# Finishing the convolution branch (LayerNorm, SiLU and gate) in the tail of the input projection instead of in the output phase

## The chip, the cores and the metric

The kernel runs on one core of one Trainium2 chip. The time is device microseconds for one execution. The engines are named as the profile names them: PE is the matrix engine (TensorE, with PEld its weight loads), DVE the vector engine, ACT the scalar engine, POOL GpSimd; SP is the queue from which most DMAs are issued, and POOL's own queue issues some.

## The reference

One decoder block, for 2048 tokens of 1024 channels in float32. The lines that matter here:

```
proj = h @ w_in[l]
a_val, a_glu, a_gate, cq, ckv, k_pe, b_gate, g_a, g_b = jnp.split(proj, split_points, axis=-1)
u = a_val * jax.nn.sigmoid(a_glu)
u = causal_depthwise_conv(u, conv_w[l], conv_b[l])          # 31 taps, per channel
u = jax.nn.silu(layer_norm(u, conv_ln_w[l], conv_ln_b[l]))  # over the 1024 channels
y_a = (u * jax.nn.silu(a_gate)) @ w_conv_out[l]
...
y_b = (o * jax.nn.silu(b_gate)) @ w_attn_out[l]
merged = jax.nn.sigmoid(g_a) * y_a + jax.nn.sigmoid(g_b) * y_b
x = x + gate[:, None, :] * (merged @ w_out[l])
```

Every large matrix product is made in three passes (`split3`, L50 to L54: high by high, high by low, low by high), since both operands are split into a rounded part (`hi`, made on ACT) and its remainder (`lo`, made on POOL or DVE).

## The kernel before, in words

Five phases run one behind the other: setup, projection, value, attention, output. Within a phase each engine has its own program in a fixed order, and semaphores join them; an engine that waits holds up all that stands behind on it.

**Projection.** The channels lie on the 128 partitions, the tokens along the row. A tile is 128 output columns of `w_in` for all 2048 tokens, in four chunks of 512 tokens (`NC_` = 4, `TC` = 512). A chunk is 8 x 3 = 24 matmuls into one of eight PSUM banks, four of them to even tiles and four to odd ones, so a bank has to be read out before the tile after next reaches it. Five tiles of the attention's latents come first (`PRE`); then a loop over `i` = 0..7 runs six kinds of tile: `glu`, `val`, `ga`, `gb`, `agate`, `bgate`. ACT applies sigmoid, copy or SiLU to each chunk while it reads the bank (L575), into `sg` for `glu`, into `u` for `val`, and into the one stage buffer `lat[:, LT - 1]` for the four kinds that SP then stores to DRAM. ACT also rounds the weights of the tile after next (L499) behind each tile, and POOL makes their remainder (L591). POOL multiplies `u` by `sg` (L631), DVE runs the 31 taps of the convolution over `u` into `acc` (L726, L730), and SP stores `acc` to `conv_dram` (L483).

**Output.** The work goes by 96 units of 24 matmuls. Units 0 to 31 (chunks n = 0 to 3, eight units each) are the attention's product, units 32 to 63 (n = 4 to 7) the convolution's, and the last 32 are `w_out`. Each chunk needs an operand of eight 128 x 512 tiles, split on ACT (L1717) and DVE (L1816). For n = 4 to 7 the operand is computed right there, one chunk ahead: load `conv_dram` and `agate_dram`, sum over the eight tiles on DVE (`total`, L1810), mean over the partitions by a matmul with a constant matrix (L1675), subtract (L1829), square on ACT (L1731), sum again (L1810), mean, root (L1733), reciprocal (L1836), scale (L1840), SiLU on ACT (L1736), gate on POOL (L1778), and then the split. DVE does these steps at the units named in `STEP_AT`, between its reads of the output banks (L1855).

## Time and profile before

| what | value |
| --- | --- |
| median of 3 runs | 2790.12 us (2789.72 to 2791.98) |
| the profiled execution, its own time | 2792.73 us |
| its span (first to last instruction) | 2790.9 us, mean granted clock 0.974 |
| PE busy | 2605.0 us (93%) |
| DVE, ACT, POOL busy | 1685.7 (60%), 894.4 (32%), 695.1 us (25%) |
| DMA | 290.44 MB, 104 GB/s over the span |

The span is 1.8 us shorter than the profiled execution's time, which is 0.1% over the median. PE busy in 93% of the span says that time can only come from the 7% where it waits, from slow stretches of its clock, or from fewer matmuls; where the waits lie has to be read stage by stage.

### The profile page before, as it was taken

What the parts mean: (1) busy time and instruction counts of PE and PEld (TensorE: products, weight loads), DVE (VectorE), ACT (ScalarE), POOL (GpSimd) and SP (SyncE); (2) the same over time, 40 slices, a digit from 0 to 9 for tenths busy, and PEclk for the clock granted to TensorE, in tenths of its full rate; (3) what the DMA queues carried; (4) which work ended last, traced back from release to release, by engine and by line L of the source; (5) the groups of instructions that cost most, each with busy time, mean ns of one, the idle gap of its engine ahead of it and who ended that gap; (6) DMA issues with size and microseconds to landing.
All of it is one profiled execution on the core that took longest, in us unless ns stands there. A gap on an engine that the chain in (4) does not pass through costs nothing. (4 is left out here: it accounts for less than half of the span.)

```text
span 2790.9 us, 33714 instructions
## 1 busy us (share of the span) xinstructions
PE 2605.0 (93%) x12185; PEld 2138.1 (77%) x12185; DVE 1685.7 (60%) x1967; ACT 894.4 (32%) x1726; POOL 695.1 (25%) x571
## 2 busy tenths in 40 slices
PE   3699999999999999997899999999999799888998
PEld 3577888888888888885687887888788687666887
DVE  5765647382929384656467767767777226666442
ACT  3432111111111111111255555555555312323221
POOL 1232211121111111121033233233223301543522
PEclk9799999999999999998999999999999899999999
DMA  7143121221212121214712212211210455555642
GB/s 258 52 137 114 53 75 45 75 68 53 68 53 88 55 90 30 90 47 156 227 64 93 103 41 77 103 60 59 103 60 27 143 193 180 177 183 204 217 166 76
DMA packets 199659, 290.44 MB, mean 104 GB/s; under 512 B 16841, under 2 KB 127501, under 8 KB 189612
## 3 DMA queue, kind: packets, MB, share of 16 engines
q1 hardware_dynamic: 198444, 285.41, 31.1%
q0 software_dynamic: 1152, 4.19, 0.5%
q8 instruction: 39, 0.64, 0.1%
q14 instruction: 24, 0.20, 0.0%
HBM read 194.67 MB, written 94.90 MB: 104 GB/s over the span
## 5 line engine op out<-in xcount | busy, mean ns | idle before, releaser
L52 PE MATMUL ps_proj<-h_hi,w_hi 128*128 128x512 f32 x1696 | 666.3, 393 | 10.8 <-POOL w_lo L591 10.8
L53 PE MATMUL ps_proj<-h_lo,w_hi 128*128 128x512 f32 x1696 | 662.5, 391 | 0.0
L54 PE MATMUL ps_proj<-h_hi,w_lo 128*128 128x512 f32 x1696 | 662.3, 391 | 0.0
L730 DVE SCALAR_TENSOR_TENSOR acc<-u,taps_t,acc 128x2048 f32<-128x2048 f32 x240 | 610.1, 2542 | 35.9 <-DVE acc L730 2.4
L591 POOL TENSOR_TENSOR w_lo<-raw,w_hi 128x1024 fp32r<-128x1024 f32 x55 | 169.8, 3088 | 884.6 <-ACT w_hi L499 884.6
L52 PEld LDWEIGHTS ps_proj<-h_hi,w_hi 128*128 128x128 f32 x1696 | 320.2, 189 | 79.1 <-POOL w_lo L591 11.0
L53 PEld LDWEIGHTS ps_proj<-h_lo,w_hi 128*128 128x128 f32 x1696 | 320.3, 189 | 67.8 <-issue 1.7
L54 PEld LDWEIGHTS ps_proj<-h_hi,w_lo 128*128 128x128 f32 x1696 | 320.0, 189 | 66.8
L1459 POOL TENSOR_SCALAR prob<-prob,rinv 128x512 f32<-128x512 f32 (+2 forms) x320 | 196.7, 633 | 355.3 <-DVE rinv L1413 355.2
L1418 DVE TENSOR_TENSOR pt_lo<-ps_t,pt_hi 128x512 fp32r<-128x512 f32 (+1 forms) x320 | 194.4, 610 | 98.8 <-ACT pt_hi L1341 94.6
L575 ACT ACTIVATE lat<-ps_proj 128x512 f32<-128x512 f32 x128 | 76.8, 600 | 547.3 <-PE ps_proj L54 480.6
L1341 ACT ACTIVATE pt_hi<-ps_t 128x512 fp32r<-128x512 f32 (+1 forms) x320 | 169.7, 532 | 240.7 <-PE ps_t L1253 240.7
L726 DVE TENSOR_SCALAR acc<-u,taps_t,prm_t 128x2048 f32<-128x2048 f32 x8 | 10.8, 1347 | 369.9 <-POOL u L631 369.9
L1395 DVE TENSOR_REDUCE nmax<-ps_ring 128x1 f32<-128x512 f32 (+3 forms) x288 | 174.9, 622 | 97.6 <-PE ps_ring L1238 79.0
L52 PE MATMUL o_ps<-o_a_hi,o_w_hi 128*128 128x512 f32 x512 | 207.0, 404 | 11.3 <-DVE o_a_lo L1816 11.3
L1333 ACT ACTIVATE prob<-ps_ring,nbias 128x512 f32<-128x512 f32 (+2 forms) x320 | 195.5, 626 | 38.5 <-DVE nbias L1401 34.1
L53 PE MATMUL o_ps<-o_a_lo,o_w_hi 128*128 128x512 f32 x512 | 201.7, 394 | 0.0
L54 PE MATMUL o_ps<-o_a_hi,o_w_lo 128*128 128x512 f32 x512 | 201.0, 393 | 0.0
L1253 PE MATMUL ps_t<-ident,prob 128*128 128x128 f32 x1088 | 174.1, 276 | 13.0 <-POOL prob L1459 9.5
L1253 PEld LDWEIGHTS ps_t<-ident,prob 128*128 128x128 f32 x1088 | 132.1, 142 | 46.0 <-POOL prob L1459 10.9
L1268 PE MATMUL ps_o<-pt_hi,v_hi 128*128 128x512 f32 (+1 forms) x320 | 141.5, 442 | 0.7 <-DVE bg L1426 0.7
L1855 DVE TENSOR_TENSOR o_y<-o_ps,o_g 128x512 f32<-128x512 f32 x64 | 43.2, 685 | 149.7 <-PE o_ps L54 64.4
(185 smaller groups left out, 4216.7 us busy)
## 6 DMA issues: line engine op xcount, KB each, us to landing
qlat<-qlat_dram SPq DMA_DIRECT2D x32, 1024.0 KB, 5.2
raw<-in_w_in_dram SPq DMA_DIRECT2D x54, 512.0 KB, 6.1
wada<-in_w_ada_dram SPq DMA_DIRECT2D x8, 1024.0 KB, 12.5
ga_dram<-lat SPq DMA_DIRECT2D x8, 1024.0 KB, 5.0
gb_dram<-lat SPq DMA_DIRECT2D x8, 1024.0 KB, 5.0
agate_dram<-lat SPq DMA_DIRECT2D x8, 1024.0 KB, 5.0
bgate_dram<-lat SPq DMA_DIRECT2D x8, 1024.0 KB, 3.9
conv_dram<-acc SPq DMA_DIRECT2D x8, 1024.0 KB, 5.0
```

Source lines behind the costliest of these rows:

```text
L52: pe.matmul(out, wh, xh, start=first, stop=False)
L53: pe.matmul(out, wh, xl, start=False, stop=False)
L54: return pe.matmul(out, wl, xh, start=False, stop=last)
L591: pool.tensor_tensor(w_lo[slot][:], raw[slot][:], w_hi[slot][:].bitcast(F32), ALU.subtract).then_inc(lo_made, 1)
L730: ins = dve.scalar_tensor_tensor(acc[:], u[:, n:n + S], tap(n), acc[:], ALU.mult, ALU.add)
L1253: mm = pe.transpose(ps_t[:, n % 2, b * P:(b + 1) * P], prob[:, x:x + P], k.ident[:])
L1268: pe.matmul(out, v_hi[:, j, :], mh, start=(j == 0), stop=False)
L1333: act.activation(prob[:, x:x + width], ps[:, chunk_no[n, c] % RING, 0:width], ACT.Exp, bias=nbias[:, n:n + 1], accum_out=rsum[:, n, c:c + ...
L1341: act.activation(pt_hi[n % SLOTS][:, s], ps_t[:, n % 2, s], ACT.Copy).then_inc(t_hi, 1)
L1395: ins = dve.tensor_reduce(to, ps[:, chunk_no[n, c] % RING, 0:width], AX.X, ALU.max, negate=True)
L1418: dve.tensor_tensor(pt_lo[n % SLOTS][:, s], ps_t[:, n % 2, s], pt_hi[n % SLOTS][:, s].bitcast(F32), ALU.subtract).then_inc(t_lo, 1)
L1459: pool.tensor_scalar(prob[:, x:x + width], prob[:, x:x + width], rinv[:, n:n + 1], 1.0, ALU.mult, ALU.mult).then_inc(normed, 1)
```

## The change

The convolution branch is finished before the projection ends, and the output phase loads a ready operand from a new DRAM tensor `z_dram`.

- The 48 tiles of the projection keep their number and their work, but not their order: eight rounds of five kinds (`glu`, `val`, `ga`, `gb`, `agate`), then the eight `bgate` tiles as a tail. The hardware loops become straight code. `TAIL` is the number of the first tail tile.
- The multiplication of `val` by `sg` moves from POOL to DVE, which reads `val` from PSUM itself (`convolve`); ACT no longer touches `val`.
- After each convolution DVE updates a running mean over the tiles and a running sum of squared deviations, 2048 tokens wide (`gather`).
- In the tail, PE makes four matmuls for the mean after chunk 1 of tile TAIL + 1 and four for the variance after chunk 1 of tile TAIL + 2; DVE and ACT finish mean and root.
- Then 32 quarter tiles (128 channels x 512 tokens) pass through six pairs of buffers, laid over `u`, `acc` and `sg`: POOL's queue loads a quarter of `conv_dram` and one of `agate_dram`, DVE subtracts and scales, ACT applies SiLU (two quarters behind each chunk of tiles TAIL + 3 to TAIL + 6), DVE gates, SP stores to `z_dram`, eight quarters ahead of the `bgate` store of each tile.
- The output phase loses all LayerNorm steps for n = 4 to 7; those chunks are split like the others.
- Setup's semaphores are cleared and freed at its end, with a barrier of all engines.

```diff
-    PER = 6
-    KINDS = ["glu", "val", "ga", "gb", "agate", "bgate"]
+    KINDS = ["glu", "val", "ga", "gb", "agate"]
+    TILES = [(kind, i) for i in range(H) for kind in KINDS] + [("bgate", i) for i in range(H)]
...
+    TAIL = PRE + H * len(KINDS)
+    Z_SLOTS = 6
+    ZW = TC
+    N_Z = NC_ * H
+    Z_AT = 8
...
+        z_buf = [b[:, n:n + ZW] for b in (u[:, PAD:], acc, sg) for n in range(0, S, ZW)]
+        z_conv, z_gate = z_buf[:Z_SLOTS], z_buf[Z_SLOTS:]
...
+                    if tile >= TAIL + 3:
+                        for h in range(N_Z)[(tile - TAIL - 3) * Z_AT:(tile - TAIL - 2) * Z_AT]:
+                            sp.wait_ge(z_done, h + 1)
+                            sp.dma_start(k.z_dram[z_rows(h), z_cols(h)], z_conv[h % Z_SLOTS]).then_inc(z_out[h % Z_SLOTS], 16)
+                    if kind in OUTS:
+                        store_tile(OUTS[kind][i * P:(i + 1) * P, :], outs_before(tile))
+                    ready = i if kind == "val" and i else H if tile == TAIL + 1 else 0
+                    if ready:
+                        sp.wait_ge(conv_done, ready)
+                        sp.dma_start(k.conv_dram[(ready - 1) * P:ready * P, :], acc[:]).then_inc(conv_out, 16)
...
+                def ln_means():
+                    for c in range(NC_):
+                        act.wait_ge(ln_dev, c + 1)
+                        act.activation(mean[:, chunk(c)], ps[:, NC_ + c, :], ACT.Copy, scale=float(KT)).then_inc(ln_mean, 1)
+                        act.activation(sg[:, chunk(c)], sg[:, chunk(c)], ACT.Square).then_inc(ln_squared, 1)
+                def ln_roots():
+                    for c in range(NC_):
+                        act.wait_ge(ln_var_mm, c + 1)
+                        act.activation(spread[:, chunk(c)], ps[:, c, :], ACT.Sqrt, bias=k.eps[:]).then_inc(ln_root, 1)
+                def silu(h):
+                    i, s = h % H, h % Z_SLOTS
+                    act.wait_ge(z_scaled, h + 1)
+                    act.activation(z_conv[s], z_conv[s], ACT.Silu, scale=k.prm_t[:, R_LNW + i:R_LNW + i + 1],
+                                   bias=k.prm_t[:, R_LNB + i:R_LNB + i + 1]).then_inc(z_silu, 1)
+                silu_at = [(TAIL + 2, 3)] + [(t, c) for t in range(TAIL + 3, N_TILES) for c in range(NC_) for _ in range(2)]
+                for tile in range(PRE, N_TILES):
+                    kind, i = kind_of(tile)
+                    for c in range(NC_):
+                        if kind != "val":
+                            act.wait_ge(chunk_mm, tile * NC_ + c + 1)
+                            dst = sg[:, chunk(c)] if kind == "glu" else stage[:, c, :]
+                            if c == 0 and kind == "glu" and i:
+                                act.wait_ge(val_used, i * NC_)
+                            if c == 0 and kind in OUTS:
+                                act.wait_ge(stored, 16 * (1 + stores_before(tile)))
+                            act.activation(dst, ps[:, tile % 2 * NC_ + c, :], FUNC[kind]).then_inc(chunk_out, 1)
+                        if tile == TAIL + 2 and c == 0:
+                            ln_roots()
+                        for h in range(N_Z):
+                            if silu_at[h] == (tile, c):
+                                silu(h)
+                    if tile + 2 < N_TILES:
+                        split_hi(0, tile % 2, raw_count(tile + 2), (tile + 1) * NC_)
+                    if tile == TAIL + 1:
+                        ln_means()
...
+                def load_z(h):
+                    s = h % Z_SLOTS
+                    if h >= Z_SLOTS:
+                        pool.wait_ge(z_out[s], 16 * (h // Z_SLOTS))
+                    pool.dma_start(z_conv[s], k.conv_dram[z_rows(h), z_cols(h)]).then_inc(z_in[s], 16)
+                    pool.dma_start(z_gate[s], k.agate_dram[z_rows(h), z_cols(h)]).then_inc(z_in[s], 16)
+                for tile in range(PRE, N_TILES):
+                    if tile == TAIL + 2:
+                        pool.wait_ge(conv_out, 16 * H)
+                        pool.wait_ge(stored, last_store("agate"))
+                        pool.wait_ge(stats_done, H)
+                        pool.wait_ge(ln_sum, NC_)
+                    if tile >= TAIL + 2:
+                        for h in range(N_Z)[Z_SLOTS + (tile - TAIL - 3) * Z_AT if tile > TAIL + 2 else 0:
+                                            Z_SLOTS + (tile - TAIL - 2) * Z_AT]:
+                            load_z(h)
+                    if tile + 2 < N_TILES:
+                        split_lo(tile + 3, tile % 2)
...
+                def convolve(i):
+                    for c in range(NC_):
+                        dve.wait_ge(chunk_mm, (PRE + i * len(KINDS) + 1) * NC_ + c + 1)
+                        dve.wait_ge(chunk_out, outs_before(PRE + i * len(KINDS)) + c + 1)
+                        if i and c == 0:
+                            dve.wait_ge(stats_done, i)
+                        dve.tensor_tensor(u[:, PAD + c * TC:PAD + (c + 1) * TC],
+                                          ps[:, (PRE + i * len(KINDS) + 1) % 2 * NC_ + c, :], sg[:, chunk(c)],
+                                          ALU.mult).then_inc(val_used, 1)
...
+                    dve.wait_ge(mean_step, i)
+                    dve.tensor_tensor(dev, acc[:], mean, ALU.subtract).then_inc(dev_done, 1)
+                    dve.wait_ge(dev_done, i)
+                    dve.scalar_tensor_tensor(mean, dev, 1.0 / (i + 1), mean, ALU.mult, ALU.add).then_inc(mean_step, 1)
+                    part_of = i / (i + 1)
+                    if i == 1:
+                        dve.wait_ge(part_hi_out, 16 * (2 * NC_ + 2))
+                        dve.wait_ge(part_lo_out, 16 * (2 * NC_ + 2))
+                        dve.scalar_tensor_tensor(spread, dev, part_of, dev, ALU.mult, ALU.mult).then_inc(stats_done, 1)
+                        return
+                    dve.wait_ge(mean_step, i + 1)
+                    dve.scalar_tensor_tensor(dev, dev, part_of, dev, ALU.mult, ALU.mult).then_inc(dev_squared, 1)
+                    dve.wait_ge(dev_squared, i - 1)
+                    dve.tensor_tensor(spread, spread, dev, ALU.add).then_inc(stats_done, 1)
...
+                def normalise_z(h):
+                    s = h % Z_SLOTS
+                    dve.wait_ge(z_in[s], 32 * (h // Z_SLOTS + 1))
+                    dve.wait_ge(ln_mean, NC_)
+                    dve.tensor_tensor(z_conv[s], z_conv[s], mean[:, z_cols(h)], ALU.subtract).then_inc(z_centred, 1)
+                    dve.wait_ge(z_centred, h + 1)
+                    dve.wait_ge(ln_done, h // H + 1)
+                    dve.tensor_tensor(z_conv[s], z_conv[s], spread[:, z_cols(h)], ALU.mult).then_inc(z_scaled, 1)
+                def gate_z(h):
+                    s = h % Z_SLOTS
+                    dve.wait_ge(z_silu, h + 1)
+                    dve.tensor_tensor(z_conv[s], z_conv[s], z_gate[s], ALU.mult).then_inc(z_done, 1)
+                for i in range(H):
+                    convolve(i)
+                    gather(i)
+                for c in range(NC_):
+                    dve.wait_ge(ln_mm, c + 1)
+                    dve.scalar_tensor_tensor(sg[:, chunk(c)], ps[:, NC_ + c, :], -float(KT), mean[:, chunk(c)], ALU.mult,
+                                             ALU.add).then_inc(ln_dev, 1)
+                for c in range(NC_):
+                    dve.wait_ge(ln_squared, c + 1)
+                    dve.scalar_tensor_tensor(spread[:, chunk(c)], sg[:, chunk(c)], float(KT), spread[:, chunk(c)], ALU.mult,
+                                             ALU.add).then_inc(ln_sum, 1)
+                invert(0)
+                normalise_z(0)
+                for h in range(N_Z):
+                    if h % H == H // 2 and h // H + 1 < NC_:
+                        invert(h // H + 1)
+                    if h + 1 < N_Z:
+                        normalise_z(h + 1)
+                    gate_z(h)
...
+                        if n == TAIL + 2:
+                            pe.wait_ge(ln_mean, c + 1)
+                        if n == TAIL + 3:
+                            pe.wait_ge(ln_root, c + 1)
...
+                        if n == TAIL + 1 and c == 1:
+                            ln_means()
+                        if n == TAIL + 2 and c == 1:
+                            ln_variances()
...
+    SOURCE_AT = {1: (0, 0), **{c: (c - 2, 4) for c in range(2, 2 * N + 2)}}
...
-                def conv_operand(c):
-                    j = c - N
-                    for h in range(2):
-                        t = slice(h * HALF, (h + 1) * HALF)
-                        act.wait_ge(centred, 2 * j + h + 1)
-                        if j and h == 0:
-                            act.wait_ge(lo_done, KT * c)
-                        act.activation(z[:, t, :], v[:, t, :], ACT.Square).then_inc(squared, 1)
-                    act.wait_ge(mean_mm, 2 * j + 2)
-                    act.activation(rstd[:], ps_m[:, 1, :], ACT.Sqrt, bias=k.eps[:]).then_inc(rooted, 1)
-                    for t in range(KT):
-                        act.wait_ge(scaled, 2 * j + t // HALF + 1)
-                        act.activation(z[:, t, :], v[:, t, :], ACT.Silu, scale=k.prm_t[:, R_LNW + t:R_LNW + t + 1],
-                                       bias=k.prm_t[:, R_LNB + t:R_LNB + t + 1]).then_inc(silu_done, 1)
-                    for t in range(KT):
-                        act.wait_ge(z_done, j * KT + t + 1)
-                        operand_hi(c, t, z)
```

The tail on ACT, from the last chunk of tile TAIL + 4 to the weights behind tile TAIL + 5. Each row is an instruction with its line, output and inputs; `lat<-ps_proj` is the read-out of a `bgate` chunk into the stage buffer, `prm_t` marks the SiLU of a quarter, and `w_hi` is a rounding of weights. After the change:

```order
L631 ACTIVATE lat<-ps_proj 128x512
L617 ACTIVATE u<-u,prm_t 128x512 x2
L545 ACTIVATE w_hi<-raw 128x1024
L631 ACTIVATE lat<-ps_proj 128x512
L617 ACTIVATE u<-u,prm_t 128x512
L617 ACTIVATE acc<-acc,prm_t 128x512
L631 ACTIVATE lat<-ps_proj 128x512
L617 ACTIVATE acc<-acc,prm_t 128x512
L617 ACTIVATE u<-u,prm_t 128x512
```

Two SiLUs stand behind each read-out, so a read-out that waits for the stage buffer holds up the quarters, and a quarter that is late holds up the next read-out and the weights of the tile after next. Before, there were read-outs and weights alone.

POOL in the tail, from the remainder of the weights of tile TAIL + 5 on; `L689` and `L690` issue the two loads of a quarter:

```order
L650 TENSOR_TENSOR w_lo<-raw,w_hi 128x1024
L689 DMA u<-conv_dram 128x512
L690 DMA sg<-agate_dram 128x512
L689 DMA u<-conv_dram 128x512
L690 DMA sg<-agate_dram 128x512
L689 DMA acc<-conv_dram 128x512
L690 DMA sg<-agate_dram 128x512
L689 DMA acc<-conv_dram 128x512
L690 DMA sg<-agate_dram 128x512
```

Sixteen such loads stand between one remainder of weights and the next (the first eight are shown), and each waits until the quarter six before it has been stored. Before, only the remainders and the multiplication `u<-u,sg` stood here.

DVE in the output phase for one chunk of the convolution (n = 5), before the change; `o_y<-o_ps` is the read-out of a unit:

```order
L1810 TENSOR_REDUCE o_tot<-o_v 128x512
L1855 TENSOR_TENSOR o_y<-o_ps,o_g 128x512
L1829 TENSOR_TENSOR o_v<-o_v,o_ps_m 128x2048 x2
L1855 TENSOR_TENSOR o_y<-o_ps,o_g 128x512
L1810 TENSOR_REDUCE o_tot<-o_z 128x512
L1855 TENSOR_TENSOR o_y<-o_ps,o_g 128x512
L1836 RECIPROCAL o_tot<-o_tot 128x512
L1840 TENSOR_TENSOR o_v<-o_v,o_tot 128x2048 x2
L1855 TENSOR_TENSOR o_y<-o_ps,o_g 128x512 x2
L1816 TENSOR_TENSOR o_a_lo<-o_z,o_a_hi 128x512 x4
L1855 TENSOR_TENSOR o_y<-o_ps,o_g 128x512
L1816 TENSOR_TENSOR o_a_lo<-o_z,o_a_hi 128x512 x4
```

and after it, where the same stretch reads:

```order
L1898 TENSOR_TENSOR o_a_lo<-o_v,o_a_hi 128x512 x8
L1910 TENSOR_TENSOR o_y<-o_ps,o_g 128x512 x8
L1898 TENSOR_TENSOR o_a_lo<-o_v,o_a_hi 128x512 x8
L1910 TENSOR_TENSOR o_y<-o_ps,o_g 128x512 x8
L1898 TENSOR_TENSOR o_a_lo<-o_v,o_a_hi 128x512 x8
```

All steps of the LayerNorm are gone from it, and the split of a chunk stands in one piece, as it did for n = 0 to 3.

## Rows read from the trace of the kernel before

**Rows 1.** Busy time by stretch: us from the start, PE, PEld, DVE, ACT, POOL, granted clock, DMA.
```profile
270.00:1294.00 1024.00, 1023.96 (x4518) 847.83 (x4516) 618.35 (x248) 178.38 (x255) 178.41 (x55) 1.00 0.21 64
...
2202.00:2332.00 130.00, 129.24 (x563) 106.87 (x564) 41.00 (x55) 24.03 (x38) 16.81 (x8) 0.98 0.63 207
2332.00:2544.00 212.00, 174.43 (x713) 137.33 (x712) 148.28 (x80) 68.20 (x76) 85.04 (x51) 0.92 0.53 179
```
**Rows 2.** PE's own waits in the output phase: who for whom, total us, times, longest.
```profile
PEld o_ps_m L1675 <- DVE o_tot L1810: 41.0, 8, 11.0
PEld o_ps L52 <- POOL o_w_lo L1771: 11.7, 2, 11.4
```
**Rows 3.** The chain that ended last, first convolution chunk: start us, us, what.
```profile
2340.26 7.32 DVE o_tot L1810
2347.62 1.12 PE o_ps_m L1675 x2
...
2357.84 0.82 ACT o_z L1736
```
**Rows 4.** Matmuls of the output phase: durations min/median/max ns, first and last start us.
```profile
L52 PE MATMUL o_ps<-o_a_hi,o_w_hi x512: 387/389/1415, 2202.8 to 2606.5; 128*128 128x512 f32 x171
...
L54 PE MATMUL o_ps<-o_w_hi,o_a_lo x256: 388/389/389, 2607.6 to 2781.2; 128*128 128x512 f32 x128
```
**Rows 5.** Timeline of ACT, projection's loop: start us, us, what, [idle before <-releaser].
```profile
309.36 0.60 ACT L575 ACTIVATE lat<-ps_proj 128x512 f32<-128x512 f32 x1 [4.84 <-PE ps_proj L54]
314.80 0.60 ACT L575 ACTIVATE lat<-ps_proj 128x512 f32<-128x512 f32 x1 [4.84 <-PE ps_proj L54]
315.29 1.05 ACT L499 ACTIVATE w_hi<-raw 128x1024 fp32r<-128x1024 f32 x1
320.61 0.60 ACT L575 ACTIVATE lat<-ps_proj 128x512 f32<-128x512 f32 x1 [4.26 <-DMA ga_dram<-lat]
...
331.12 0.60 ACT L575 ACTIVATE lat<-ps_proj 128x512 f32<-128x512 f32 x1 [4.84 <-PE ps_proj L54]
```
**Rows 6.** Timeline of DVE and SP: the first convolution and its store.
```profile
301.13 1.35 DVE L726 TENSOR_SCALAR acc<-u,taps_t,prm_t 128x2048 f32<-128x2048 f32 x1 [30.71 <-POOL u L631]
...
383.51 0.37 SPq L483 DMA_DIRECT2D conv_dram<-acc  x1
```
**Rows 7.** DVE groups by form: count, busy us, mean ns, idle before.
```profile
L1840 DVE TENSOR_TENSOR o_v<-o_v,o_tot 128x2048 f32<-128x2048 f32 x8 | 18.0, 2287 | 0.1
...
L1836 DVE RECIPROCAL o_tot<-o_tot 128x512 f32<-128x512 f32 x4 | 13.4, 3350 | 4.6 <-ACT o_tot L1733 4.6
```
**Rows 8.** Timeline of DVE and of POOL, two places.
```profile
2236.08 4.90 DVE L1816 TENSOR_TENSOR o_a_lo<-o_v,o_a_hi 128x512 fp32r<-128x512 f32 x8
...
338.18 3.80 POOL L591 TENSOR_TENSOR w_lo<-raw,w_hi 128x1024 fp32r<-128x1024 f32 x1 [18.43 <-ACT w_hi L499]
```
**Rows 9.** Timeline of SP: the projection's last issues, the value phase's first.
```profile
1294.62 0.37 SPq L439 DMA_DIRECT2D bgate_dram<-lat  x1
1297.11 0.37 SPq L483 DMA_DIRECT2D conv_dram<-acc  x1
1301.44 0.95 SPq L827 DMA_DIRECT2D wv_raw<-in_w_ukv_dram  x2
```
**Rows 10.** DMA issues: count, KB each, median us from issue to landing.
```profile
bgate_dram<-lat SPq DMA_DIRECT2D x8, 1024.0 KB, 3.9
...
bg<-bgate_dram SPq DMA_DIRECT2D x32, 256.0 KB, 2.6
...
o_v<-conv_dram SPq DMA_DIRECT2D x8, 1024.0 KB, 7.9
...
o_yb<-yb_dram SPq DMA_DIRECT2D x32, 256.0 KB, 4.6
```
**Rows 11.** Timeline of POOL: its own DMA issues, the first and a later one.
```profile
112.59 1.66 POOL L600 DMA_DIRECT2D wada_gate<-in_w_ada_dram  x1
...
199.25 0.90 POOL L600 DMA_DIRECT2D wada_gate<-in_w_ada_dram  x1
```

272 lines of the change are left out of this document (102 added, 170 removed).

## The prediction

> **What bounds the kernel now.** I read the busy time by stretch first. In the projection (270 to 1294 us) PE is busy for all of it at full clock, while DVE, ACT and POOL have 406, 846 and 846 us to spare [rows 1]. There anything given to them is free as long as it never holds PE up, and anything given to PE is paid in full. In the output phase PE is busy through the attention's product, and from 2332 to 2544 us, where the operands of the convolution are made, it is busy for only 174.4 of 212 us at a mean granted clock of 0.92 [rows 1]. PE's own waits there are 41.0 us before the mean matmuls, for DVE's sums, and 11.7 us for weights that POOL made late [rows 2]. The chain of work that ended last runs through the same steps: a sum of 7.32 us on DVE, a pair of mean matmuls of 1.12 us, SiLU and gate [rows 3].
>
> **How much the output phase can lose.** A chunk takes PE 5.44 us: ACT's read-outs of two chunks one whole tile apart begin at 309.36 and 331.12, so a tile is 21.76 us and a chunk of 24 matmuls a quarter of it [rows 5]. The output phase is 96 such units, 522.2 us. Its matmuls start at 2202.8, and the last starts at 2781.2, 0.2 us before its slot ends: 578.6 us [rows 4]. Of the excess of 56.4 us, 2.4 belong to the slow clock at its beginning (0.98 of 130 us [rows 1]), which stay. That leaves **54 us**, with the eight mean pairs (9 us) in it.
> Does something take their place? Chunks 4 to 7 get the program of chunks 0 to 3, which kept PE waiting for nothing after its start. Their operand loads fall from 3 MB to 1 MB a chunk, and POOL and ACT lose gate, squares and SiLU. The one crowded place is the start of chunk 4, where eight pieces of weights are fetched two per unit from unit 27 on. A piece costs landing, 1.05 us on ACT [rows 5] and 2.4 to 3.8 on POOL [rows 8], two buffers deep, so some 5 us; the eight are done some 43 us after the first is asked for, and PE needs the last 27 + 38 = 65 us after it. Covered by 20 us. I take all 54; the lower bound is 52.
>
> **What the projection gains in work.**
> - Mean and variance: eight matmul pairs move here. A pair lasts 1.12 us alone [rows 3], of which about 0.15 overlaps its neighbour: **8 us** (7.2 to 9), all on PE's path.
> - The mean's return: tile TAIL + 2 may not start before ACT has read the mean of chunk 0. ACT does so behind the last read-out of tile TAIL + 1 and the rounding of weights. The read-out begins about 0.2 us after PE could go on (a matmul takes 389 ns, the next starts 227 ns behind it [rows 4, 5]), the rounding 0.49 after that and takes 1.05, the mean's copy 0.6 [rows 5]: 2.3 us and a semaphore, **2.4 us**. The roots do not cost that: they are made in the middle of tile TAIL + 2 and wanted at its end, 10.9 us later.
> - Barrier and clearing between the phases: the last store of the projection lands at 1297.11 + 3.9 = 1301.0 and the next phase's first issue is at 1301.44 [rows 9, 10], so a barrier is 0.4 us. I take **0.6**, to 1.5.
> - DVE in the rounds: a convolution runs from 301.13 to 383.51, 82.4 us [rows 6], waits and clashes with POOL included. The statistics are four passes of 2048 elements, two at 2.29 [rows 7], two like a tap at about 2.5, with semaphores 9.9, and up to 1 for a clash: 10.8. With the last multiplication (0.9) that is 94 us of the 108.8 us of five tiles. The first chunk of the next `val` comes 92.5 us after the end of the last: DVE is 1.5 us late for it and in time for the next. That costs nothing, since the bank is wanted a tile and a half later. If cover were gone, each us beyond 108.8 would cost eight.
> - The statistics in time: counted from the start of the tail, S0, the eighth `val` ends at -65.3, and the sums are ready at -65.3 + 94.1 = 28.8. PE asks for them after six chunks, at 32.6. In time by 3.8 us.
>
> **The tail, where I expect a new wait.** Per quarter DVE has a subtraction and a scaling that wait for each other (0.68 + 0.05 each, estimated from a run of eight tiles in 4.90 us, so 0.60 each in a row [rows 8]) and a gate (0.60): 2.1 us; per eight quarters 16.5 us, a reciprocal of 3.35 [rows 7] and 2.4 us of standing still while POOL makes weights: 22.3, already a bit over a tile. Then comes the loop that the order on SP and ACT makes. SP stores the `bgate` tile only behind the eighth quarter of that tile; the first read-out of the next tile waits for this store, and its two SiLUs stand behind the read-out, while DVE may work only one quarter ahead. So from the gate of quarter 7 to that of quarter 15 it takes two issues (0.8), the landing b of 1024 KB, read-out and SiLU (0.6 + 0.82 [rows 3, 5]), and then DVE's remaining 18.4 us with 0.3 of semaphores: **20.9 + b**. Between 3.9 us, the same store in a quiet loop, and more than 7.9 us, a load of the same size in the output phase [rows 10], b is nearest to the latter: eight quarters move 6 MB, with weights and `bgate` 7.5 MB, in 29 us some 270 GB/s, over the 207 and 179 of those stretches [rows 1]. I take 8.5: 29.4 us per eight quarters, against PE's 21.76.
> Tile TAIL + 3 ends on PE at 4 x 21.76 + 8 + 2.4 = 97.4; the gate of quarter 7 is done at 99.6, that of 23 at 158.4. POOL may load quarter 29 only when 23 is stored (issue 0.4, landing as `yb` 4.6 [rows 10]), needs two issues of 0.90 [rows 11], and only then makes the weights of the last tile (3.0): 158.4 + 10.1 = 168.5. PE has finished the last tile but one at 7 x 21.76 + 10.4 = 162.7. It waits **5.8 us** (with b = 3.9 not at all; each us of b is two).
> The Trainium skill, DMA: Bandwidth & Descriptors, section Anatomy of one DMA, gives a transfer 2.0 us plus its bytes at 436 GB/s, 4.4 us for this store and 2.6 for a quarter; by it b were 4.4, PE would not wait in the tail, and the sum would be that of rival A. The rows agree where the chip is quiet (3.9, and 2.6 for 256 KB) and not under traffic (7.9) [rows 10].
> - The end: until now the last convolution's store ended the phase (1297.11 + 3.9); now the `bgate` store does, issued at 1294.62, landed at 1298.5 [rows 9, 10]. **2.5 us** are gained. Quarter 31 is done some 24 us after quarter 23, before PE ends.
>
> **Sum.** -54 + 8 + 2.4 + 0.6 + 5.8 - 2.5 = -39.7 us. The profiled execution's 2792.73 us is 0.1% over the median of 2790.12; taken from the median, this gives 2750.
>
> **Rivals.**
> - A, the tail hides everything: b near 3.9. No wait for the last tile, 2790.1 - 45.5 = 2745; with the smallest bounds 2743. For it speaks that 16 transfers of 256 KB are little for queues that moved 207 GB/s without holding PE up. Chance 0.2.
> - B, the quarters are slower still: six pairs of buffers make a round of store, landing, two loads, landing, two DVE passes, SiLU and gate. With 0.4 + 4.6 + 1.8 + 7.9 + 1.5 + 0.8 + 0.7 = 17.7 us a quarter comes every 2.95 us, just behind DVE's share of my loop; if landings double, or an issue takes 1.66 us [rows 11] and b is 12, eight quarters take 33 to 37 us, the last weights come 12 to 20 us late, and the stores behind the last quarter add up to 6: 2757 to 2772. Chance 0.26.
> - C, statistics late: if POOL and DVE clash on every pass, `gather` takes 19 us, PE waits 4.4 us once, 2755. Chance 0.05.
> - D, slower than before: the gain is used up when the last tile's wait passes 5.8 + 39.7 = 45.5 us, that is quarter 23 at 198 and 49 us per eight, 6.1 us per quarter. One mechanism could do it: a store of a quarter stuck in SP's order behind the `bgate` store, so that loads, which wait for it, run in turn and not side by side; one round of buffers would have to take 37 us in place of 17.7. With both at once the time is 2795 or more. Chance 0.04.
>
> **How the numbers follow.** The forecast (2746 to 2756) has 0.45, A 0.2, B 0.26, C 0.05, D 0.04. The range of eight in ten begins at A's bound, 2743, and reaches to B's end, 2772. A measurement of this kernel tells 0.2%, 5.6 us, from no change. Only D is not faster by that: faster 0.94, same 0.02, slower 0.04.
>
> **What would show it.** Right: from the output phase's first matmul to its last some 524 us and no wait on PE over 2 us; in the projection two groups of four mean pairs, a wait of 2 to 3 us before tile TAIL + 2, and one before the last tile for POOL's `w_lo`; eight quarters every 28 to 31 us; `bgate` landings near 8 us in the tail. Wrong: waits of PE for a `val` bank in the rounds (DVE over 108.8 us), or for the sums at S0 + 32.6; waits at the start of chunk 4; or quarters that keep PE's pace, which is A.

## The result, and the profile after

| kernel | median | ratio to before, 95% interval |
| --- | --- | --- |
| before | 2789.92 us (2787.59 to 2791.98, 4 runs) | |
| after | 2743.12 us (2742.82 to 2745.5, 4 runs) | 0.9834 (0.9817 to 0.9851) |

The change saves 46.8 us, 1.7%; 2750 was forecast, 39.7 saved in the sum. The profiled execution of after took 2742.87 us with a span of 2741.1, against 2790.9 before. The spans differ by 49.8 us, 3 more than the medians, because the profiled execution of before was 2.8 us over its median.

Busy time of after by stretch (columns as in [rows 1]): the projection behind the latents, its tail, and the two parts of the output phase.

```profile
270.00:1301.00 1031.00, 1028.79 (x4525) 848.93 (x4525) 821.19 (x416) 189.70 (x262) 183.96 (x110) 1.00 0.28 89
1130.00:1301.00 171.00, 168.79 (x731) 136.83 (x730) 99.62 (x115) 55.44 (x80) 48.63 (x70) 1.00 0.64 212
2207.00:2337.00 130.00, 129.52 (x564) 107.15 (x565) 34.57 (x55) 23.74 (x38) 16.77 (x7) 0.98 0.59 192
2337.00:2549.00 212.00, 212.00 (x937) 175.61 (x936) 60.23 (x79) 35.08 (x53) 68.72 (x42) 1.00 0.67 214
```

The last row answers to the 174.43 busy us of 212 in [rows 1]: the operands of the convolution now cost PE nothing, and its clock stays at full speed. DVE is busy for 821 us in the projection, a third more than the 618 in [rows 1], and PE stood still for only 2.2 us there. The tail moves 212 GB/s over its length, 280 in its middle (1245 to 1273 us).

The matmuls of the output phase, first kind and last (durations, then first and last start):

```profile
L52 PE MATMUL o_ps<-o_a_hi,o_w_hi x512: 387/389/766, 2207.5 to 2556.8; 128*128 128x512 f32 x171
...
L54 PE MATMUL o_ps<-o_w_hi,o_a_lo x256: 388/389/389, 2558.0 to 2731.4; 128*128 128x512 f32 x128
```

From the first to the last it is 523.9 us, against 578.4 in [rows 4]: 54.5 less. The two rows in [rows 2] are of PEld, the weight loads. PE's own rows, before, in the output phase:

```profile
PE o_ps_m L1675 <- DVE o_tot L1810: 37.5, 7, 10.5
PE o_ps L52 <- DVE o_a_lo L1816: 11.3, 1, 11.3
```

So 37.5 of the 54.5 us are PE's waits for the sums. The other 17 are left for the eight pairs of mean matmuls and for the slow clock (0.92 in [rows 1], 1.00 now); how they share was not measured. The wait of 11.3 us lies ahead of the phase's first matmul and is still there after the change, at 11.5.

PE's waits after the change, from 250 to 1340 us:

```profile
PE ps_v L52 <- DMA ckv_lo<-ckv_dram: 15.7, 1, 15.7
PE ps_proj L52 <- ACT lat L606: 2.2, 1, 2.2
PE ps_v L52 <- DVE wv_lo L1059: 1.2, 1, 1.2
```

Two of the three belong to the next phase's start. In the projection one wait is left, for the mean (L606), and none before the last tile, where 5.8 us were forecast.

How the 49.8 us are made up, from the starts of the matmuls of each phase:

| part | before | after | difference |
| --- | --- | --- | --- |
| start to first projection matmul | 110.4 | 111.0 | +0.6 |
| first to last projection matmul | 1183.2 | 1190.5 | +7.3 |
| last projection matmul to first of the value phase | 17.3 | 16.0 | -1.3 |
| value and attention, to the output's first | 891.9 | 890.0 | -1.9 |
| output phase, first to last matmul | 578.4 | 523.9 | -54.5 |
| last matmul to the end | 9.7 | 9.7 | 0 |

The 7.3 us are two groups of mean matmuls (6.9), the wait (2.4), and 2.0 less in the five latent tiles, whose work the change does not touch. From the first matmul to the end of these tiles it took 138.9 and 138.5 us in the two profiles with the old projection, 136.8 to 137.3 in eleven of twelve with the new one, and 139.4 in the twelfth (`slots5_lo`). So most of it repeats; its cause is open.

### The profile page after: what moved, and what is told of

It is laid out like the page before. It is cut to its first block and busy times, and to the rows that moved or that the text cites. A ratio compares the mean times of both kernels' runs of the same rounds, so it can differ in the third digit from the quotient of the medians.

```text
span 2741.1 us, 32651 instructions
## 1 busy us (share of the span) xinstructions
PE 2592.6 (95%) x12185; PEld 2132.1 (78%) x12185; DVE 1757.6 (64%) x2107; ACT 853.9 (31%) x1686; POOL 642.4 (23%) x593
## 5 line engine op out<-in xcount | busy, mean ns | idle before, releaser
L52 PE MATMUL ps_proj<-h_hi,w_hi 128*128 128x512 f32 x1696 | 666.6, 393 | 13.6 <-POOL w_lo L650 11.4
L810 DVE SCALAR_TENSOR_TENSOR acc<-u,taps_t,acc 128x2048 f32<-128x2048 f32 x240 | 629.0, 2621 | 8.5
L52 PE MATMUL o_ps<-o_a_hi,o_w_hi 128*128 128x512 f32 x512 | 200.0, 391 | 11.5 <-DVE o_a_lo L1898 11.5
L1910 DVE TENSOR_TENSOR o_y<-o_ps,o_g 128x512 f32<-128x512 f32 x64 | 43.9, 690 | 258.9 <-PE o_ps L54 190.7
L1401 PE MATMUL ps_ring<-kn_hi,qn_hi 128*128 128x512 f32 (+2 forms) x320 | 125.3, 392 | 8.5 <-ACT prob L1501 5.0
## 6 DMA issues: line engine op xcount, KB each, us to landing
wada<-in_w_ada_dram SPq DMA_DIRECT2D x8, 1024.0 KB, 12.7
```

Of the source, the lines that this page charges most:

```text
L52: pe.matmul(out, wh, xh, start=first, stop=False)
L810: dve.scalar_tensor_tensor(acc[:], u[:, n:n + S], tap(n), acc[:], ALU.mult, ALU.add).then_inc(conv_tap if n < TAPS - 1 else conv_done, 1)
```

## Experiments

All ratios are to the kernel before, run on the same chip as the experiment. Lines and buffers have the names of after; where an edit adds lines, the line numbers behind it move by a few. A quarter is counted by its number, 0 to 31, and "gate 7" is the start of DVE's gate multiplication of quarter 7. In the code, `...` stands for lines left out.

### The two halves of the change by themselves

`out_alone` is the kernel before with only the output phase replaced, fed with raw data:

```
-        sources = [by_tile(ap) for ap in (k.attn_dram, k.z_dram, k.merged_dram)]
+        sources = [by_tile(ap) for ap in (k.attn_dram, k.conv_dram, k.merged_dram)]
```

> Leaves out the convolution's LayerNorm, SiLU and gate: the projection is that of before, the output phase that of after, fed with conv_dram. Theory (the gain is the waits of the output phase, and the projection gives back its share of work): the output phase runs 524 us from first to last matmul, 54.5 less than before, so 2735 to 2736 us, ratio 0.9805. Rival (the new projection itself gains something, for instance by the new order of its tiles, and the output phase less than 54): 2738 or more.

Measured: 2736.7 us (2733.89 to 2737.05), ratio 0.9804 (0.9787 to 0.9822). Its output phase from first to last matmul:

```profile
L52 PE MATMUL o_ps<-o_a_hi,o_w_hi x512: 389/389/767, 2201.6 to 2551.0; 128*128 128x512 f32 x171
...
L54 PE MATMUL o_ps<-o_w_hi,o_a_lo x256: 388/389/389, 2552.1 to 2725.5; 128*128 128x512 f32 x128
```

That is 523.9 us, the same as in after.

`proj_alone` has the other half: setup and projection of after, the output phase of before, so that LayerNorm, SiLU and gate are made twice and `z_dram` is written in vain.

> The projection of after with the output phase of before, which makes LayerNorm, SiLU and gate a second time from conv_dram; z_dram is written and not read. Theory: the projection costs 6.9 us for the mean matmuls, 2.4 for the wait before tile TAIL + 2, 0.6 for the barrier, and gains 1.3 at its end and up to 2 in the latent tiles: 2790 + 7 = 2797 us (2795 to 2799). Rival (the new projection is no dearer than the old, since the tail hides all but the matmuls and the order gains elsewhere): 2790 to 2793.

Measured: 2796.98 us (2795.67 to 2802.34), ratio 1.0033 (1.0023 to 1.0042), against 2789.02 for before: 8.0 us dearer. So the halves add up: -52.3 and +8.0 give -44.3, and after measured -46.8 above and -44.8 when it was repeated (below). The whole gain lies in the output phase, and the projection gives back about a seventh of it. One caution on its size: the output phase of before, which stands unchanged in `proj_alone`, took 574.9 us from first to last matmul there and 578.4 in the profile of before. The gain is therefore 51.0 to 54.5 us, by which of the two is taken.

### Leaving the quarters out

`no_quarters` drops the 32 quarter tiles, their loads, both DVE passes, SiLU, gate and stores; it keeps statistics, mean matmuls and reciprocals, and the output phase reads `conv_dram`.

```
-                    if tile >= TAIL + 3:      # SP: stores of quarters
+                    if False:
...
-                    if tile >= TAIL + 2:      # POOL: loads of quarters
+                    if False:
...
-                    gate_z(h)                 # DVE; likewise normalise_z(h), and silu(h) on ACT
```

> Leaves out the 32 quarter tiles (their loads, centring, scaling, SiLU, gate and stores); statistics, mean matmuls and reciprocals stay, and the output phase reads conv_dram. Theory (all quarters lie beside PE's work, and the phase ends with PE): the time stays, 2743 us, 2741 to 2745. Rival (the quarters cost PE time somewhere, by DMA traffic, by the phase's end or by the value phase behind it): the time falls by more than 3 us, to below 2740.

Measured: 2742.14 us (2741.07 to 2744.31), ratio 0.9833 (0.9817 to 0.985), beside 0.9834 of after. The intervals of the two ratios are 4.7 us wide to each side, so the medians alone do not exclude the rival's 3 us. The profiles do: from the projection's first to its last matmul `no_quarters` took 1192.4 us and after 1190.5, and from there to the value phase's first 14.6 and 16.0. Even without the 1.6 us of slow clock that this profile of `no_quarters` has behind its wait (see below), the quarters cost about 1 us. So the rival is out: 24 MB of traffic, 96 DVE operations and 32 SiLUs are nearly free, and what is paid is the statistics and what they make PE wait for.

### How much room the tail has: fewer buffers

`slots5` and `slots3` change one number:

```
-    Z_SLOTS = 6
+    Z_SLOTS = 5      # and 3
```

> Five pairs of buffers for the quarter tiles in place of six. Theory (eight quarters are paced by the loop of bgate store, read-out and SiLU, 27 to 28 us; a round of the buffers is only some 14 us, 0.4 + 4.5 store, 1.1 + 5.5 loads, 1.4 + 0.8 + 0.6 for the passes, so 2.9 us a quarter with five): the time stays within 1 us of 2743. Rival (the buffers pace the quarters): eight quarters take 6/5 of 27.4, 32.9 us, quarter 23 is 15 us later, and past a margin of 0.7 us PE waits for it: 2757.

> Three pairs of buffers. Theory: now the round of the buffers, 14.3 us, is the pace: 4.8 us a quarter, 38 us for eight in place of 27.4. Quarter 23 is some 32 us later (11 for the first eight, 10.5 for each of the next two), of which a margin of 0.7 us is hidden and the rest is PE's wait for the last tile's w_lo; quarter 31 then ends some 10 us behind PE's last tile and holds the phase's end: 2743 + 31 + 10 = 2784 us (2775 to 2792). Rival (the buffers pace the quarters already with six): 55 us for eight, 2820 or more. Second rival (the last weights do not depend on the quarters): 2743 to 2755.

Measured: `slots5` 2751.48 us (2750.38 to 2753.2), ratio 0.9861 (0.9843 to 0.9878); `slots3` 2806.47 us (2803.02 to 2809.18), ratio 1.0057 (1.0037 to 1.0077). Both missed their theory, and both lie between theory and rival. PE's waits, first of `slots5`, then of `slots3`, from 250 to 1340 us:

```profile
PE ps_v L52 <- DMA ckv_lo<-ckv_dram: 14.3, 1, 14.3
PE ps_proj L52 <- POOL w_lo L650: 7.0, 1, 7.0
PE ps_proj L52 <- ACT lat L606: 2.2, 1, 2.2
```

```profile
PE ps_proj L52 <- POOL w_lo L650: 43.9, 2, 22.9
PE ps_proj L52 <- ACT lat L606: 2.2, 1, 2.2
```

The new wait is where it was looked for, at the weights of the last tiles. The size was off because the round of a buffer is longer than the 14.3 us that the expectations used. In `slots3` the gates of quarters 7, 15 and 23 start at 1229.2, 1274.8 and 1320.0, so eight quarters take 45.4 us and a round of three buffers 17.0. That is the 17.7 of the prediction's rival B, which the expectations had wrongly shortened. With six buffers a round of 17.0 gives 22.7 us for eight quarters; with five 27.2, as much as the loop of `bgate` store and read-out needs (27.4 and 28.3 in after). Gates 7, 15 and 23 stand at 1216.8, 1246.2 and 1275.5 in `slots5`, 29.4 and 29.3 us apart, more than either. That two limits of the same size get in each other's way is an explanation that no run here tests. What the last weights wait for is seen on POOL in `slots5`:

```profile
1276.81 0.54 POOL L689 DMA_DIRECT2D u<-conv_dram  x1 [0.29 <-DMA z_dram<-u]
1277.51 0.54 POOL L690 DMA_DIRECT2D acc<-agate_dram  x1 [0.16 <-issue]
1283.46 0.54 POOL L689 DMA_DIRECT2D u<-conv_dram  x1 [5.42 <-DMA z_dram<-u]
1283.99 0.54 POOL L690 DMA_DIRECT2D sg<-agate_dram  x1
1284.55 2.35 POOL L650 TENSOR_TENSOR w_lo<-raw,w_hi 128x1024 fp32r<-128x1024 f32 x1
```

The load at 1283.46 waits for the store of quarter 23. That store was issued at about 1276.2, when its gate had ended, so it took 7.2 us to land. In after the same place looks like this:

```profile
1275.69 0.54 POOL L689 DMA_DIRECT2D acc<-conv_dram  x1
1276.21 0.54 POOL L690 DMA_DIRECT2D sg<-agate_dram  x1
1276.77 2.41 POOL L650 TENSOR_TENSOR w_lo<-raw,w_hi 128x1024 fp32r<-128x1024 f32 x1
```

The store was issued at 1272.65 (the second of a pair of SP issues that begins at 1270.71 and ends 2.25 later, less 0.32) and had landed by 1275.69, within 3.0 us. The weights end at 1279.18; PE begins the last tile at 1301.4 + 0.2 - 21.76 = 1279.9. The margin is 0.7 us.

The time of `slots5` is 8.4 us over that of after, and the projection of its profile is 10.0 us longer: the 7.0 of the wait and about 3 of the slow clock behind it (below), less 1.3 that the phase's end gives back. In `slots3` the projection is 50.3 us longer than in after and the way to the value phase 12.7, 63 together, which is the difference of the times.

### The order on POOL

`slots5_lo` keeps five buffers and moves the weights ahead of half of the loads:

```
                             load_z(h)
-                    if tile + 2 < N_TILES:
+                            if tile > TAIL + 2 and tile + 2 < N_TILES and (h - Z_SLOTS) % Z_AT == Z_AT // 2 - 1:
+                                split_lo(tile + 3, tile % 2)
+                    if tile <= TAIL + 2:
                         split_lo(tile + 3, tile % 2)
```

> Five pairs of buffers as in slots5 (where PE waited 7.0 us for w_lo of the last tile), and POOL makes the weights of tiles TAIL + 6 and TAIL + 7 behind four of the eight quarters' loads and not behind all eight. Theory (PE's wait comes only from the order on POOL, where the weights stand behind loads that wait for the store of quarter 23): w_lo is made 7 us earlier, right behind w_hi, the wait falls to 0 to 1 us, quarters keep their pace: about 2744 to 2746, with 1 to 2 us left at the phase's end, where quarter 31 is 8 us later than with six. Rival (the weights are late because ACT rounds them late, behind its SiLUs): the wait stays at 5 us or more and the time at 2750.

Measured: 2756.47 us (2755.57 to 2757.97), ratio 0.9887 (0.9871 to 0.9904). PE's wait for the weights fell from 7.0 to 1.7 us, as the theory had it, and yet the time is no shorter than that of `slots5`. The medians are 5 us apart, but the two intervals overlap a little and the chips differ, and the profiles put these 5 us where the edit does not reach: 2.5 in the latent tiles and 2.8 between value and output. What the edit reaches comes out even. Behind the latent tiles the projection is 8.1 us shorter (1055.5 and 1063.6), by the wait and the slow clock behind it, and the way to the value phase's first matmul is 7.9 longer. POOL's timeline shows why:

```profile
1243.93 0.54 POOL L689 DMA_DIRECT2D u<-conv_dram  x1 [4.03 <-DMA z_dram<-u]
1244.45 0.54 POOL L690 DMA_DIRECT2D acc<-agate_dram  x1
1251.96 2.39 POOL L650 TENSOR_TENSOR w_lo<-raw,w_hi 128x1024 fp32r<-128x1024 f32 x1 [6.96 <-ACT w_hi L545]
1254.30 0.55 POOL L689 DMA_DIRECT2D u<-conv_dram  x1
```

The wait was turned round: the second half of the loads now stands behind weights that wait for ACT, and ACT rounds only behind its eight SiLUs. So from the gate of quarter 7, at 1220.4, to that of quarter 8, at 1231.8, 11.4 us pass, against 6.3 in `slots5`. The end of the phase slips, and the value phase's first matmul comes 22.6 us behind the projection's last, against 14.7 in `slots5`. So the order on POOL is the cause of PE's wait, and taking it away in this manner costs as much again at the phase's end.

### The `bgate` store ahead of the eighth quarter

`bgate_first` moves one store on SP:

```
+                            if h % Z_AT == Z_AT - 1:
+                                store_tile(OUTS[kind][i * P:(i + 1) * P, :], outs_before(tile))
                             sp.wait_ge(z_done, h + 1)
...
-                    if kind in OUTS:
+                    if kind in OUTS and not TAIL + 3 <= tile < TAIL + 7:
                         store_tile(OUTS[kind][i * P:(i + 1) * P, :], outs_before(tile))
```

> In SP's order the bgate store of a tail tile stands ahead of the eighth quarter's store of that tile, not behind it. Theory (the loop of bgate store, read-out and two SiLUs paces the quarters): the store leaves some 2 us earlier in the first such tile and 3 to 5 in the others, the gate of quarter 15 comes 2 us earlier and that of 23 5 us; PE had no wait, so the time stays within 1 us of 2743. Rival (the store of quarter 23 now lies behind 1 MB in the queues and lands later, by 4 us or more, than the gate gains): w_lo of the last tile is late, PE waits 1 to 4 us and the time is 2744 to 2747.

Measured: 2743.81 us (2740.91 to 2748.17), ratio 0.9846 (0.9829 to 0.9862): no difference to after. Gates 15 and 23 start at 1242.2 and 1267.6, so eight quarters take 25.7 and 25.4 us in place of 27.4 and 28.3: the loop through the store was indeed the pace. But the gain is not margin, since the first half of the rival holds too: the store of quarter 23 was issued at 1268.29 behind the 1 MB of `bgate` and landed at 1275.32, after 7.0 us in place of 3.0, and POOL began the weights at 1276.40, where it is 1276.77 in after. PE's wait, the rival's second half, did not come in this profile.

### The mean earlier

`mean_early` moves ACT's part of the mean into a place where ACT has nothing to do:

```
+                        if tile == TAIL + 1 and c == 1:
+                            ln_means()
...
-                    if tile == TAIL + 1:
-                        ln_means()
```

> ACT copies the mean and squares the deviations behind the second read-out of tile TAIL + 1, where it stands idle for 8 us, and not behind the fourth read-out and the rounding of weights. Theory: PE's wait of 2.4 us before tile TAIL + 2 goes, and everything behind it moves up by as much, quarters too, since they start behind PE's variance matmuls: no new wait at the last tile, 2740.7 us. Rival (the quarters keep their times, as their pace is set by stores and not by PE): PE waits 2.4 - 0.7 = 1.7 us before the last tile and the time is 2742.5.

Measured: 2739.11 us (2738.12 to 2741.03), ratio 0.9825 (0.9809 to 0.9842). ACT's timeline:

```profile
1150.87 0.60 ACT L631 ACTIVATE lat<-ps_proj 128x512 f32<-128x512 f32 x1 [4.52 <-PE ps_proj L54]
1152.46 0.60 ACT L606 ACTIVATE lat<-ps_proj 128x512 f32<-128x512 f32 x1 [0.99 <-DVE sg L859]
...
1155.94 0.65 ACT L607 ACTIVATE sg<-sg 128x512 f32<-128x512 f32 x1
1159.75 0.60 ACT L631 ACTIVATE lat<-ps_proj 128x512 f32<-128x512 f32 x1 [3.16 <-PE ps_proj L54]
```

The eight operations fit between two read-outs. PE has no wait left in the projection from 250 us on. Everything behind moved up with PE, as the theory had it: gate 0 from 1194.4 to 1191.7, gate 23 from 1271.9 to 1267.1. The difference to after was 4.0 us, not 2.4; in the profiles 2.5 of it lie in the projection.

### The clock behind a wait

The three kernels below ran on one chip, five executions each. `bf_mean` is `mean_early` and `bgate_first` in one.

> The changed kernel once more, on the chip of the two below. All theories: 0.9834 of before within 0.0015, about 2743 us.

> mean_early once more, beside the changed kernel. Theory: PE's wait of 2.6 us before tile TAIL + 2 is gone and nothing takes its place: 2.5 to 4 us below after_again. Rival (the 4.0 us between the medians so far were mostly chance): less than 1.5 us below it.

> mean_early with the bgate store of tiles TAIL + 3 to TAIL + 6 ahead of the eighth quarter's store. Theory (quarters are hidden, so quicker quarters add only margin): the time of mean_again within 1 us, the gate of quarter 23 4 us earlier than there. Rival (quicker quarters end the phase sooner): 1 to 2 us below mean_again.

| kernel | median | ratio |
| --- | --- | --- |
| `after_again` | 2743.75 (2742.76 to 2748.5) | 0.9843 (0.9829 to 0.9856) |
| `mean_again` | 2741.38 (2739.5 to 2744.85) | 0.9834 (0.982 to 0.9847) |
| `bf_mean` | 2745.76 (2740.41 to 2747.67) | 0.9843 (0.9829 to 0.9856) |

`mean_again` is 2.4 us below `after_again`, short of the 2.5 that its theory asked for, and the intervals overlap; `bf_mean` went against both theories. The stretch from 1165 to 1174 us, in after, `after_again` and `mean_again`:

```profile
1165.00:1174.00 9.00, 6.79 (x30) 5.37 (x29) 3.78 (x4) 6.25 (x12) 2.54 (x2) 1.00 0.80 273
```

```profile
1165.00:1174.00 9.00, 6.79 (x23) 5.12 (x22) 3.78 (x4) 5.57 (x10) 2.39 (x1) 0.81 0.77 263
```

```profile
1165.00:1174.00 9.00, 9.00 (x42) 7.44 (x41) 0.00 (x0) 3.43 (x4) 2.39 (x1) 1.00 0.76 260
```

The busy time is the same in the first two, 6.79 us, but 23 matmuls ran in it and not 30, at a granted clock of 0.81. Behind PE's stand of 2.4 us, which follows a stretch in which PE was never idle, the clock fell from 2.4 to 1.2 GHz for about 3 us in `after_again` (matmuls 0.43 us apart in place of 0.23), and also in `no_quarters`, `proj_alone` and `slots3` (0.81 over 9 us), but not in after, `slots5`, `bgate_first` and `slots5_lo`. Seven matmuls at 0.227 us are 1.6 us. So this wait costs 2.4 us in some executions and 4 in others; without it, as in `mean_again`, the clock stayed full. The two profiled executions show the sum: from the projection's first to its last matmul 1193.2 us in `after_again` and 1188.2 in `mean_again`, 5.0 less, which are the wait, the clock and 0.8 before the last tile. Behind the 7.0 us in `slots5` the granted clock from 1277 to 1290 us was 0.72.

The other unsteady thing is the store of quarter 23. POOL in `mean_again`, then in `bf_mean`:

```profile
1274.31 0.54 POOL L689 DMA_DIRECT2D acc<-conv_dram  x1 [2.85 <-DMA z_dram<-acc]
```

```profile
1277.03 0.54 POOL L691 DMA_DIRECT2D acc<-conv_dram  x1 [6.84 <-DMA z_dram<-acc]
```

and SP's issues in `bf_mean`:

```profile
1265.45 0.32 SPq L525 DMA_DIRECT2D z_dram<-acc  x1
1265.82 0.43 SPq L481 DMA_DIRECT2D bgate_dram<-lat  x1
1267.38 0.32 SPq L525 DMA_DIRECT2D z_dram<-acc  x1
```

Issued at 1267.38 behind the `bgate` store, it landed 9.65 us later, and PE waited 2.4 us for the last weights although the gate was earlier than in `mean_again`. Ahead of the `bgate` store it took at most 3.0 us in after, 5.0 in `mean_again`, 5.6 in `after_again` (where PE waited 0.8 us) and 7.2 in `slots5`. So one and the same kernel waits in some executions and not in others.

The stores right behind the `bgate` store were slower still, in after as well. SP and POOL there:

```profile
1217.29 0.43 SPq L481 DMA_DIRECT2D bgate_dram<-lat  x1
1217.77 0.45 SPq L444 DMA_DIRECT2D raw<-in_w_in_dram  x1
1218.86 9.32 SPq L523 DMA_DIRECT2D z_dram<-u  x2
```

```profile
1222.09 0.54 POOL L689 DMA_DIRECT2D u<-conv_dram  x1 [3.13 <-DMA z_dram<-u]
...
1232.28 0.55 POOL L689 DMA_DIRECT2D u<-conv_dram  x1 [6.71 <-DMA z_dram<-u]
```

The first load waits for quarter 7, stored just ahead of `bgate`: 5.2 us. The second waits for quarter 8, issued at 1218.86 behind `bgate` and the 512 KB of the next weights: 13.4 us. In all five profiles with this order and six buffers (after, `after_again`, `mean_early`, `mean_again`, `proj_alone`) the stores of quarters 8 and 16 took 12.5 to 13.9 us, that of quarter 24, with no weights between, 8.7 to 9.2, and those of quarters 7, 15 and 23 3.0 to 6.2.

### The weights ahead of one load

`mean_lo1` is `mean_early`, and POOL's order is that of `slots5_lo` with `Z_AT - 2` for `Z_AT // 2 - 1`: only the load that needs the store of quarter 23 stands behind the weights.

> mean_early with six pairs of buffers and POOL making the weights of tiles TAIL + 5 plus 1 and plus 2 ahead of the last of the eight quarters' loads, the only one that waits for the store of quarter 23 (or 15, or 7). Theory (what threatens PE is the landing of that one store, 3 to 10 us in the profiles so far): w_lo of the last tile then depends on the store of quarter 22 and on ACT's w_hi; it is made 3 us or more before PE wants it, the last load is not later than before, and the time is that of mean_early and mean_again, 2739 to 2741.5, 0.9825 to 0.9834 of before, with no wait of PE in the tail. Rival (as in slots5_lo, a load behind the weights waits for ACT's rounding and slows the quarters, and the phase ends later): over 2744.

Measured: 2743.13 us (2740.95 to 2745.04), ratio 0.9836 (0.9822 to 0.9849). POOL at the end:

```profile
1269.78 0.54 POOL L690 DMA_DIRECT2D sg<-agate_dram  x1
1270.33 2.41 POOL L650 TENSOR_TENSOR w_lo<-raw,w_hi 128x1024 fp32r<-128x1024 f32 x1
1272.99 0.55 POOL L689 DMA_DIRECT2D acc<-conv_dram  x1 [0.25 <-DMA z_dram<-acc]
```

The weights end at 1272.7, and PE begins the last tile at 1299.3 + 0.2 - 21.76 = 1277.7: the margin is 5 us in place of 0.7, the quarters are not slower (gate 23 at 1267.2, gate 31 at 1290.3), and PE waits nowhere in the tail. The mechanism is as the theory had it. The time is between theory and rival, and the intervals of `mean_early`, `mean_again`, `mean_lo1` and after all overlap. The part from the value phase's first matmul to the output's first, which none of these kernels touches, took between 889.1 and 892.9 us in the profiles of `mean_early`, `mean_again`, `mean_lo1`, after, `after_again` and `bf_mean`; that alone hides a gain of 2 to 4 us. None of these is shown to beat after; all of them beat the kernel before.

## Why the prediction was right, and where not

The terms as the profiles have them are -54.5 + 6.9 + 2.4 + 0.6 - 1.3 - 2.0 - 1.9 = -49.8 us, the difference of the spans. The mechanism of the gain is the one forecast. The time is not where the sum put it: 2743.1 lies below the forecast's own 2746 to 2756 and only 0.1 us inside the range of eight in ten, and that it lies inside is luck.

- **Output phase, -54:** -54.5 in after; `out_alone` has the same 523.9 us. Against the other profile of the old phase it is -51.0. Nothing took the place of the waits, not at the start of chunk 4 either. One reading was wrong: the 11.7 us that the prediction placed among the waits from 2332 us on are, but for 0.3, the wait ahead of the phase's first matmul. The sum is not touched, since the 54 came from first to last matmul.
- **Mean matmuls, +8:** 6.9. The term was mis-sized: a pair was taken as 1.12 us less 0.15 of overlap. In a group of four pairs each matmul starts 0.43 us behind the one before, so that a group takes 3.4 us:

```profile
L888 PE MATMUL ps_proj<-lat,mean_mat x8: 591/592/592, 1150.9 to 1153.9; 128*128 128x512 f32 x8
```

- **The mean's return, +2.4:** 2.37 between two matmuls (2.60 less the usual 0.23). The way to it was right too, since moving ACT's eight operations took it away. Not foreseen was the clock behind it, up to 1.6 us more.
- **Barrier, +0.6:** 0.6. The first matmul of the projection starts at 110.4 and 110.1 us in before and `out_alone`, and at 110.9 to 111.4 in all profiles with the new setup.
- **DVE in the rounds, statistics in time:** both right. PE waited for no `val` bank, with taps of 2.62 us on average; the last pass of the statistics ended at 1146.4, and PE asked at 1150.7: 4.3 us of margin, 3.8 forecast. Rival C did not come about.
- **The wait before the last tile, +5.8:** none in after and 0.8 in its repetition. This is the step that failed. Its mechanism is right in the main: the loop through the `bgate` store was the pace (`bgate_first`), it reaches PE through POOL's order (`slots5_lo`, `mean_lo1`), and the price b was right as well. ACT's timeline of after:

```profile
1217.05 1.04 ACT L545 ACTIVATE w_hi<-raw 128x1024 fp32r<-128x1024 f32 x1
1225.81 0.60 ACT L631 ACTIVATE lat<-ps_proj 128x512 f32<-128x512 f32 x1 [7.71 <-DMA bgate_dram<-lat]
1226.30 0.81 ACT L617 ACTIVATE u<-u,prm_t 128x512 f32<-128x512 f32 x1
...
1254.28 0.60 ACT L631 ACTIVATE lat<-ps_proj 128x512 f32<-128x512 f32 x1 [8.75 <-DMA bgate_dram<-lat]
```

  The stores were issued at 1217.29 and 1244.73, so with 0.4 for the issue b was 8.1 and 9.1 us (8.5 forecast). What was too long is the rest: from the read-out to the gate of the last quarter of a tile it took 17.8 and 17.7 us (1225.81 to 1243.65, 1254.28 to 1271.93), where 20.1 were forecast. DVE's 2.4 us of standing still beside POOL's weights had been added, but they fell into time in which DVE waited for the store anyhow. On the other side the loop holds a wait that was not forecast:

```profile
1238.46 0.69 DVE L844 TENSOR_TENSOR u<-u,lat 128x512 f32<-128x512 f32 x1 [1.63 <-DMA sg<-agate_dram]
```

  This is quarter 14, whose loads had to wait for the store of quarter 8 and its 13.4 us; in the next cycle quarter 22 waits 1.43 us behind that of quarter 16 in the same way. So the buffers already added 1.4 to 1.6 us to each cycle with six pairs. (The prediction does not say how its 18.4 us are made up, so the rest of that difference cannot be assigned.) A cycle was 27.4 and 28.3 us and not 29.4. Counted from the tail's start at 1118.2, the gate of quarter 7 was done 0.9 us earlier than forecast and that of quarter 23 4.0 us earlier. Behind it 6.6 us passed from the gate's end to the end of `w_lo` and not 10.1 (the terms named there add up to 9.8): an issue of POOL's took 0.54 and not 0.90, `w_lo` 2.41 and not 3.0, and the landing at most 3.0 with its issue and not 5.0. So the weights were ready 7.5 us earlier than forecast, PE wanted them 1.0 us earlier, and the 5.8 us of wait became 0.7 of margin.
- **The end, -2.5:** -1.3. The last `bgate` store was issued at 1302.54 and the next phase's first load at 1307.49, so it took 4.6 us to land where the 3.9 of a quiet loop was taken. Another 0.6 lies behind that load: from it to the value phase's first matmul it took 10.0 us, and 9.4 before.
- **Not in the sum:** 2.0 us in the latent tiles and 1.9 in value and attention, which the change does not touch. The second is within the 3.8 us by which that part differs between profiles; the cause of the first is open.
- **Rivals:** A, the tail hides everything, is what happened: 2745 forecast, 2743.1 measured, at its lower bound; it had 0.2. It was right for another reason than its own (b was not near 3.9). B came about with fewer buffers only: its round of 17.7 us measured 17.0 in `slots3`, and the step in time lies between six and five. D came about in `slots3`: slower than before once eight quarters took 45.4 us, where 49 were forecast; the wait was 43.9 us, against the 45.5 at which it was to decide, and the phase's end added the rest.

The rule of the Trainium skill, DMA: Bandwidth & Descriptors, section Anatomy of one DMA, that was weighed against the rows gives, as an estimate, 4.4 us for the `bgate` store and 2.6 for a quarter. The section states it for transfers issued from GpSimd's queue; the stores here are issued from SP, so the prediction stretched it. The loads of a quarter, which POOL issues, took 4.6 to 6.9 us in after (medians). For the stores the median landing of after is

```profile
bgate_dram<-lat SPq DMA_DIRECT2D x8, 1024.0 KB, 5.0
...
z_dram<-u SPq DMA_DIRECT2D x22, 256.0 KB, 4.5
```

and under 280 GB/s in the tail's middle 8.1 to 9.1 for the first. The estimate fits the last store, at 4.6, and not those that set the pace; the time came out as it would have by the rule, because the rest of the loop and the way behind it were shorter.

## What to carry to other kernels

Move work off the engine that the end hangs on into a stretch where another engine stands idle, and count only what the bound engine itself has to do and to wait for: here 24 MB of traffic and 128 operations cost about 1 us, while 16 matmul instructions and one wait, 9.3 us, are more than the 8 that the projection became dearer. When a cycle is summed, do not add a clash to it that falls into the cycle's own wait. Before calling a tail hidden, measure the margin at the one instruction that ties it to the bound engine, and see which landing it hangs on: a load that waits for a store, with the next weights behind it in the same queue, turns a late landing into a stand of PE, while one load moved behind the weights gave 5 us of room without slowing the quarters, and four moved behind them, with five buffers, took PE's wait away and gained no time.
